# First gathered rows in the places of keys, values and attention probabilities, with two weight blocks loaded there afterwards

## The chip, the cores and the metric

The kernel runs on one core of a Trainium2 chip, in one launch. The metric is the device time of one execution in microseconds (us); the number compared is the median of the runs. The chip's core has a tensor engine (PE), a vector engine (DVE), a scalar engine (ACT), GpSimd (POOL), a sync engine (SP) that only issues transfers here, and 16 DMA engines that carry every transfer, whoever issued it.

## The reference, cut to what matters

Two transformer blocks for 256 tokens of width 1024, in float32. The change lies in the second one, at the seam between its attention and its last part, `peer`: each token picks 16 of 16,384 experts for each of 8 heads, and for each pick one row of `u` and one of `v` (1024 numbers each) is fetched.

```python
def peer(h, w_query, sub_keys, u_tab, v_tab):
    q = rmsnorm((xt @ w_query).reshape(T, PEER_HEADS, 2, PEER_PK_DIM))
    s = jnp.einsum('thpd,pnd->thpn', q, sub_keys)
    s1, i1 = lax.top_k(s[:, :, 0], PEER_TOPK)
    s2, i2 = lax.top_k(s[:, :, 1], PEER_TOPK)
    ...
    best, pos = lax.top_k(cand, PEER_TOPK)
    eidx = jnp.take_along_axis(cidx, pos, axis=-1)
    gate = jax.nn.softmax(best, axis=-1)
    ...
        act = jax.nn.gelu(jnp.einsum('td,thkd->thk', xb, u_tab[ib])) * gb
        return jnp.einsum('thk,thkd->td', act, v_tab[ib])
```

Before it stand, for both halves of 128 tokens, the attention (`diff_attention`, heads by keys and values), the products with `w_branch_attn`, `w_branch_sgu` and `w_out`, and a norm.

## The kernel before, in words

All of on-chip memory that matters is one tensor `AR` with 128 partitions, cut up by hand. `o = W0 + 4096` is an offset in it. From `o` lie the keys `KX` (2048 numbers), from `o + 2048` the values `VX` (2048), from `o + 16384` the probabilities `PP`, and from `o + 18432` further attention scratch (`TT`, `AA` and the start of `ATT`). All four are last used by the last attention product, the event ("mm", "av", 15).

The second block is worked in an order written out by hand, `ORDER`, a list of stages that every engine walks through, each taking the stages that are its own. The first half of the tokens (a = 0) is carried through to `peer` first. Then come 256 "rows": row (ix, k) is the gather of one expert row for each of 128 tokens, 16 rows (k) for each of 16 pairs of half and head (ix). Row number n is 16·ix + k. The rest of the second half's mixer (a = 1) is laid between the rows by the table `late`: after row 12 stage hn1, after row 22 the product `ba` 0 (with `w_branch_attn`, first block), after row 26 `ba` 1 (second block), after rows 34 and 38 `op` 0 and 1 (with `w_out`), then the query products `qm` and the routing (`rt0` to `rt5`) of later heads.

A row goes through four engines. POOL issues the gather (L2128) once the indices of its head are there ("ei", ix) and its place is free. DVE multiplies the first 1024 numbers with the token and sums (L1695). For each pair of rows ACT computes the gate and two diagonal matrices (L2057, L2063). PE multiplies the second 1024 numbers into the sum (L1027, 32 small matmuls for a pair, event ("mm", "row", ix, p)); with that the places of both rows are free. ACT, DVE and PE keep to the order of the list, so a stage that waits holds back the rows behind it.

`row_places()` plans where each row lands. It keeps a list of places of 2048 numbers, takes the first, notes what frees it, and puts it at the end. Ahead of row 0 the list holds the halves of three weight slots (free once `wq` 0, `w_bs` 0 1 and `w_bs` 1 1 have been used) and the place `o + 21504`: seven places, so row n goes where row n - 7 was. More come in at `yt` 1 (after row 30) and later.

SP issues the weight loads in its own part, in order. At the stage `take` 0 it issues the last two blocks of `w_branch_sgu`, the first two of `peer_w_query`, and then, after ("mm", "av", 15), three blocks for the second half of the tokens: `w_branch_attn` 0 at `W0`, `w_branch_attn` 1 at `o` (both key and value places) and `w_out` 0 at `o + 16384`. Each is 2048 KB. The next load on SP after them is `w_out` 1, which waits for the use of `w_branch_attn` 0; the blocks of `peer_w_query` follow.

Of the kernel before, what the change touches and what calls it, by code (L numbers as in the profile page):

```python
# [14 lines left out]
NS = 6  # L15
# [106 lines left out]
def build(nc, D, out):  # L122
    from contextlib import ExitStack
    ctx = ExitStack()
    with ctx:
# [48 lines left out]
        o = W0  # L174
# [10 lines left out]
        o = W0 + 4096  # L185
# [25 lines left out]
        o = W0 + 4096  # L211
# [41 lines left out]
        def weight(name, n):  # L253
            return D[name][n].rearrange("p (j n) -> p j n", j=8)
# [101 lines left out]
        def expert_order():  # L356
            todo, pre = [], 0
            for dc in range(4):
                pieces = [(m, n, q) for m, q in AHEAD[dc] for n in range(2)]
                total, done = len(pieces), 0  # L360
                for b in range(16):
                    if dc < 3:
                        upto = total * (b - 2) // 13 if b > 2 else 0
                    else:
                        upto = (9 * (b - 2) // 5 if b < 8 else 9 + 9 * (b - 7) // 8) if b > 2 else 0
                    here = pieces[done:upto]
                    news = [(m, q) for m, n, q in here if n == 0]
                    if dc < 3:
                        for x in news:
                            todo.append(("pre", pre, *x))  # L370
                            pre += 1
                    todo.append(("down", dc, *divmod(b, 4)))
                    if dc == 3:
                        for x in news:
                            todo.append(("pre", pre, *x))
                            pre += 1
                    if b % 4 == 0 and b + dc:
                        todo.append(("spread", *divmod(4 * dc + b // 4 - 1, 4)))
                    if b == 2 and dc:
                        todo.append(("turn", dc - 1))  # L380
                    todo += [("piece", *x) for x in here]
                    done = upto
                assert done == total
            todo += [("bias",), ("spread", 3, 3), ("biasb",)]
            return todo

        PHASE = expert_order()
        ROWS = {}

        def row_places():  # L390
            halves = [[NARENA + i * SLOT, NARENA + i * SLOT + 2048] for i in RING]
            free = {}
            for i, event in ((2, ("wq", 0, 0)), (0, ("w_bs", 0, 1)), (1, ("w_bs", 1, 1))):
                free.update({k: ("used", *event) for k in halves[i]})
            bufs = list(free)
            for stage, *x in ORDER:
                new = {}
                if (stage, *x) == ("bs", 1, 1):
                    new[o + 21504] = ("zn", 1)
                elif (stage, *x) == ("yt", 1):  # L400
                    new[o + 2048] = ("used", "w_ba", 1, 1)
                elif (stage, *x) == ("qme", 3, 1):
                    new = {k: ("used", "wq", 1, 0) for k in halves[3]}
                elif (stage, *x) == ("rt0", 8):
                    new = {o + 16384: ("used", "wq", 0, 1), o + 18432: ("used", "wq", 0, 1), W0 + 2048: ("used", "wq", 3, 0)}
                free.update(new)
                bufs += new
                if stage == "row":
                    k = bufs.pop(0)
                    ROWS[(*x,)] = k, free[k]  # L410
                    free[k] = ("mm", "row", x[0], x[1] // 2)
                    bufs.append(k)

        row_places()

        def tensor(pe, w):
# [596 lines left out]
            def v_step(ix, p):  # L1015
# [3 lines left out]
                for r in range(2):  # L1019
                    k = 2 * p + r  # L1020
                    off, _ = ROWS[ix, k]
                    w.wait_ge("landed", ix, k)
# [25 lines left out]
            def last_row(k):  # L1048
                off, _ = ROWS[15, k]
                for m in range(2 if k == 12 else 0):  # L1050
                    _, before = banks.use("leave", 1, m)
                    w.wait_ge(*before)
                w.wait_ge("last", k)
                w.wait_ge("landed", 15, k)
                for m in range(2):
                    x = pe.matmul(PS[:, banks.at("leave", 1, m), :], LAST[:, k - 12, :], AR[:, off + 1024 + m * 512:off + 1536 + m * 512],
                                  start=(k == 12), stop=(k == 15), skip_group_check=True)
                    if k == 15:
                        x.then_inc(*w.hit("mm", "leave", 1, m))
# [11 lines left out]
        def vector(v, w):  # L1071
# [617 lines left out]
            def row(ix, k):  # L1689
                a, h = work[ix]  # L1690
                off, _ = ROWS[ix, k]
                rows = AR[:, off:off + 1024]
# [408 lines left out]
        def gpsimd(pool, w):  # L2101
# [22 lines left out]
            def row(ix, k):  # L2124
                off, free = ROWS[ix, k]
                w.wait_ge("ei", ix)
                w.wait_ge(*free)
                pool.indirect_dma_start(out=AR[:, off:off + 2048], out_offset=None, in_=D["peer_uv_2"],  # L2128
                                        in_offset=bass.IndirectOffsetOnAxis(ap=EI[:, ix, k:k + 1], axis=0)).then_inc(
                    *w.hit(f"row{off}", ix, k, also=[("landed", ix, k)], by=16))  # L2130
# [7 lines left out]
        def sync(sp, w):  # L2138
            user, turn, ids = {}, [0], [list(range(NS))]

            def load(slot, key, src, *shape, count=None):
                n = 1
                for s in shape:
                    n *= s
                dst = AR[:, place[slot]:place[slot] + n]
                if len(shape) == 2:
                    dst = dst.rearrange("p (a b) -> p a b", a=shape[0])
                elif len(shape) == 3:
                    dst = dst.rearrange("p (a b c) -> p a b c", a=shape[0], b=shape[1])
                IN[key] = dst  # L2150
                if slot in user:
                    w.wait_ge("used", *user[slot])
                own = COUNT.get(slot, slot) if count is None else count
                sp.dma_start(dst, src).then_inc(*w.hit(f"slot{own}", *key, also=[("in", *key)], by=16))
                user[slot] = key

            def ring(key, src, *shape):
                slot = ids[0][turn[0] % len(ids[0])]
                turn[0] += 1
                load(slot, key, src, *shape)  # L2160
# [83 lines left out]
            for stage, *x in ORDER:  # L2244
                if stage == "rest" and (x[1] == 0 or x[0] not in ("k", "v")):
                    ring(("w_in2", x[0], x[1]), D["w_in_2"][PAIRS.index(x[0]), 3].rearrange("p (n j c) -> p n j c", n=2, j=2), 2, 2, 512)
                elif stage == "zn1" and x[0] == 0:
                    w.wait_ge("mm", "y", 3)
                    load(NS + 2, ("rows",), D["rows"].partition_broadcast(128), 2, 1024)
                elif stage == "bs" and x[1] == 0:  # L2250
                    square(("w_bs", *x), "w_branch_sgu_2", x[0])
                elif stage == "take" and x[0] == 0:
                    for n in range(2):
                        square(("w_bs", n, 1), "w_branch_sgu_2", n)
                    assert turn[0] % 4 == 2
                    for n in range(2):
                        square(("wq", n, 0), "peer_w_query_2", n)
                    w.wait_ge("mm", "av", 15)
                    for slot, key, name, n in ((NS, "w_ba", "w_branch_attn_2", 0), (NS + 4, "w_ba", "w_branch_attn_2", 1),
                                               (NS + 5, "w_op", "w_out_2", 0)):  # L2260
                        load(slot, (key, n, 1), weight(name, n), 8, 512)
                    turn[0], ids[0] = 0, [NS, NS + 5]
                elif stage == "ba" and x[1] == 0:
                    square(("w_ba", *x), "w_branch_attn_2", x[0])
                elif stage == "op" and x != [0, 1]:
                    square(("w_op", *x), "w_out_2", x[0])
                elif stage == "qm" and x in ([4, 0], [6, 0], [0, 1]):
                    square(("wq", x[0] // 2, x[1]), "peer_w_query_2", x[0] // 2)
                elif stage == "leave":
                    a = x[0]  # L2270
                    for m in range(2):
                        f = slice(m * 512, (m + 1) * 512)
                        w.wait_ge("out", a, m)
                        sp.dma_start(out[a * 128:(a + 1) * 128, f], OUTS[a][:, f]).then_inc(*w.hit("stored", a, m, by=16))
# [133 lines left out]
```

## Time and profile before

| | |
|---|---|
| median of 3 runs | 2083.95 us (2083.92 to 2088.63) |
| profiled execution, its own time | 2088.11 us |
| span of the profile | 2086.3 us |
| mean granted clock of the tensor engine | 0.81 |
| PE busy, DVE busy, ACT busy, POOL busy | 71%, 37%, 21%, 15% of the span |
| DMA, whole span | 800.00 MB, 383 GB/s on average |

The busy shares are means over stages with quite different limits. Times below are from the start of the span. The first row is issued at 1402.0 us; what comes before and after is to be read in stretches.

### The profile page before, as it was taken

To read this page: it belongs to the slowest core of one execution; us is meant where nothing else is said; L and a number is where in the kernel's file an instruction comes from. 1 tells how busy PE (TensorE), PEld (TensorE's weight loads), DVE (VectorE), ACT (ScalarE), POOL (GpSimd) and SP (SyncE) were. 2 spreads that over 40 slices of the span, in tenths; PEclk is the share of its full clock that TensorE was granted. 3 is DMA by queue.
4 is the path that set the end of the run, shared out by engine and by line. 5 is a ranking of instruction groups with operands and counts; after the bars stand their busy time and mean duration, and the time that the engine had idled before them with its cause. 6 is when DMAs were issued, how large, how long until landed. Compare 5 with 4: busy or idle time off the path is not lost.

```text
span 2086.3 us, 27127 instructions
## 1 busy us (share of the span) xinstructions
PE 1476.3 (71%) x11468; PEld 647.3 (31%) x11468; DVE 782.1 (37%) x1941; ACT 430.1 (21%) x1013; POOL 304.8 (15%) x290
## 2 busy tenths in 40 slices
PE   9999566877565555689899999986767744444444
PEld 7654122422111112234334445563235410000001
DVE  5832010000000000000122265547767677867764
ACT  1331100000000000011000145643245622221212
POOL 0010000000000000000000000004344444544441
PEclk9999788888878887799999999997788855555556
DMA  9798999999999999999998754469999999999997
GB/s 406 287 404 369 388 428 428 426 429 427 428 427 429 427 428 426 423 406 419 404 414 347 296 187 146 164 261 390 415 422 420 420 420 421 421 421 420 421 421 304
DMA packets 78057, 800.00 MB, mean 383 GB/s; under 512 B 9232, under 2 KB 9360, under 8 KB 10736
## 3 DMA queue, kind: packets, MB, share of 16 engines
q1 hardware_dynamic: 40304, 529.61, 60.9%
q0 software_dynamic: 37632, 268.65, 31.1%
q8 instruction: 91, 1.49, 0.3%
q14 instruction: 30, 0.25, 0.0%
HBM read 796.98 MB, written 1.05 MB: 383 GB/s over the span
## 4 chain that ended last, share of the span: by engine, by line
PE 42%; DMA 41%; DVE 9%; ACT 3%; issue 2%; POOL 2%; SPq 0%; DVEq 0%; ACTq 0%; POOLq 0%
DMA AR<-in_peer_uv,AR 14%; DMA AR<-in_w_gate 10%; DMA AR<-in_w_up 10%; PE PS L811 6%; PE PS L745 6%; DMA AR<-in_w_down 5%; PE PS L443 4%; PE PS L776 4%; DVE AR L1695 3%; PE PS L454 3%; PE PS L891 2%; POOL AR L2128 2%; PE PS L1027 2%; PE PS L984 2%; PE PS L707 1%
## 5 line engine op out<-in xcount | busy, mean ns | idle before, releaser
L745 PE MATMUL PS<-AR 128*32 128x512 f32 x2048 | 316.0, 751 | 200.4 <-DMA AR<-in_w_up 110.8
L1027 PE MATMUL PS<-AR 32*32 32x512 f32 x4032 | 225.5, 931 | 289.8 <-ACT AR L2063 289.7
L2128 POOL DMA_INDIRECT AR<-in_peer_uv,AR x256 | 288.8, 1128 | 967.4 <-DVE AR L1686 665.3
L1695 DVE CUSTOM_DVE_ANT_0 AR<-AR 128x1024 f32<-128x1024 f32 x256 | 309.3, 1222 | 161.7 <-DMA AR<-in_peer_uv,AR 161.3
L1323 DVE TENSOR_TENSOR AR<-AR,PS 128x512 f32<-128x512 f32 x16 | 11.0, 688 | 571.9 <-PE PS L745 571.9
L745 PEld LDWEIGHTS PS<-AR 128*32 128x32 f32 x2048 | 63.6, 124 | 422.7 <-DMA AR<-in_w_up 173.2
L776 PE MATMUL PS<-AR 128*32 128x256 f32 x2048 | 148.1, 439 | 53.5 <-DMA AR<-in_w_down 53.5
L1027 PEld LDWEIGHTS PS<-AR 32*32 32x32 f32 x4032 | 37.4, 125 | 432.6 <-ACT AR L2063 426.9
L811 PE MATMUL PS<-AR 128*128 128x512 f32 x336 | 154.2, 602 | 0.0
L776 PEld LDWEIGHTS PS<-AR 128*32 128x32 f32 x2048 | 68.8, 123 | 139.4 <-DMA AR<-in_w_down 70.0
L443 PE MATMUL PS<-AR 128*128 128x512 f32 x224 | 102.1, 610 | 1.9 <-DVE AR L1093 1.9
L2057 ACT ACTIVATE AR<-AR 128x2 f32<-128x2 f32 x126 | 25.6, 203 | 375.9 <-DVE AR L1695 375.6
L1378 DVE TENSOR_TENSOR AR<-AR,PS 128x512 f32<-128x512 f32 x56 | 38.5, 688 | 145.6 <-PE PS L811 116.8
L2122 POOL MEMSET AR<- 128x378 f32 x1 | 0.4, 412 | 630.3 <-PE PS L745 630.3
L811 PEld LDWEIGHTS PS<-AR 128*128 128x128 f32 x336 | 61.3, 190 | 76.3 <-issue 75.8
L984 PE MATMUL PS<-AR 128*128 128x128 f32 x512 | 69.3, 300 | 5.2 <-DVE AR L1618 3.9
L984 PEld LDWEIGHTS PS<-AR 128*128 128x128 f32 x512 | 66.7, 214 | 11.4 <-issue 5.9
L2063 ACT ACTIVATE AR<-AR 128x32 f32<-128x32 f32 x252 | 67.3, 314 | 8.9
L443 PEld LDWEIGHTS PS<-AR 128*128 128x128 f32 x224 | 42.9, 196 | 57.1 <-issue 57.1
L1351 DVE COPY AR<-PS 128x256 f32<-128x256 f32 x16 | 6.8, 422 | 134.5 <-PE PS L776 134.5
L454 PE MATMUL PS<-AR 128*128 128x256 f32 x256 | 56.3, 381 | 0.5 <-DVE AR L1093 0.5
L1896 ACT COPY AR<-PS 128x512 f32<-128x512 f32 x16 | 9.3, 584 | 222.3 <-PE PS L758 222.3
(320 smaller groups left out, 1592.3 us busy)
## 6 DMA issues: line engine op xcount, KB each, us to landing
AR<-in_w_up SPq DMA_DIRECT2D x64, 2048.0 KB, 17.4
AR<-in_w_down SPq DMA_DIRECT2D x64, 2048.0 KB, 14.5
AR<-in_w_gate SPq DMA_DIRECT2D x63, 2048.0 KB, 20.9
AR<-in_w_in SPq DMA_DIRECT2D x33, 1024.0 KB, 7.4
AR<-in_w_ada SPq DMA_DIRECT2D x12, 2048.0 KB, 13.2
AR<-in_w_out SPq DMA_DIRECT2D x6, 2048.0 KB, 8.9
AR<-in_w_in SPq DMA_DIRECT2D x5, 2048.0 KB, 14.0
AR<-in_peer_w_query SPq DMA_DIRECT2D x5, 2048.0 KB, 11.5
```

The lines of the kernel that those rows point to most:

```text
L443: i = pe.matmul(PS[:, b, :], src[:, j, a * 128:(a + 1) * 128], IN[key][:, j, :], start=(j == 0), stop=(j == 7))
L454: i = pe.matmul(PS[:, b, q * 256:(q + 1) * 256], IN[key][:, j, (e + q) * 128:(e + q + 1) * 128], src[:, j, :], start=(j == 0), stop=(j == 7))
L745: x = pe.matmul(PS[32 * q:32 * q + 32, bk, :], XS[e][:, j, :], src[:, q * 512:(q + 1) * 512], start=(j == 0), stop=(j == 7), skip_group_ch ...
L776: x = pe.matmul(PS[32 * g:32 * g + 32, b, 0:256], HDT[4 * q + g][:, sh, blk * 32:(blk + 1) * 32], IN[key][:, g, sh, :], start=(blk == 0 an ...
L811: x = pe.matmul(PS[:, b, :], HT[:, 2 * q + j, a * 128:(a + 1) * 128], IN[key][:, n, j, :], start=(j == 0), stop=(j == 1))
L891: x = pe.matmul(PS[:, to[n][0], :], HT[:, j, a * 128:(a + 1) * 128], IN[key][:, n, j - 6, :], start=False, stop=(j == 7))
L984: x = pe.matmul(PS[:, b, q * 128:(q + 1) * 128], IN[key][:, j, (2 * r + q) * 128:(2 * r + q + 1) * 128], HT[:, j, a * 128:(a + 1) * 128], ...
L1027: x = pe.matmul(PS[c:c + 32, ACC[a][g], :], DI[t, p, r, :], AR[t, off + 1024 + m * 512:off + 1536 + m * 512], start=(h == 0 and p == 0), s ...
L1378: v.tensor_tensor(d, d, PS[:, banks.at("part", m, n, q, a), :], ADD).then_inc(*w.hit("summed", m, n, q, a, also=[("part", m, n, q, a)]))
L1695: v.tensor_tensor_reduce(rows, rows, HB[:, a, :], 1.0, 0.0, MULT, ADD, DOT[:, ix, k:k + 1]).then_inc(*w.hit("dot", ix, k))
L2063: i = act.activation(DI[:, p, r, :], SG2[:, ix % 2, 2 * p + r, :], ACT.Copy, scale=two[:, r:r + 1])
L2128: pool.indirect_dma_start(out=AR[:, off:off + 2048], out_offset=None, in_=D["peer_uv_2"], in_offset=bass.IndirectOffsetOnAxis(ap=EI[:, ix, ...
```

## The change

The four places of the attention become places for rows, at the head of the list. After the stage hn1 of the second half (behind row 12) they are taken out of the list again, and what frees each of them is noted in `GIVEN`. SP waits for that before it loads `w_branch_attn` 1 at `o` and `w_out` 0 at `o + 16384`; `w_branch_attn` 0, at `W0`, is loaded as before.

```diff
-        ROWS = {}
+        ROWS, GIVEN = {}, {}
 
         def row_places():
             halves = [[NARENA + i * SLOT, NARENA + i * SLOT + 2048] for i in RING]
-            free = {}
+            free = {k: ("mm", "av", 15) for k in (o, o + 2048, o + 16384, o + 18432)}
             for i, event in ((2, ("wq", 0, 0)), (0, ("w_bs", 0, 1)), (1, ("w_bs", 1, 1))):
                 free.update({k: ("used", *event) for k in halves[i]})
             bufs = list(free)
@@
+                for k in (o, o + 2048, o + 16384, o + 18432) if (stage, *x) == ("hn1", 1) else ():
+                    bufs.remove(k)
+                    GIVEN[k] = free.pop(k)
                 free.update(new)
                 bufs += new
@@
                     for slot, key, name, n in ((NS, "w_ba", "w_branch_attn_2", 0), (NS + 4, "w_ba", "w_branch_attn_2", 1),
                                                (NS + 5, "w_op", "w_out_2", 0)):
+                        for k in {NS + 4: (o, o + 2048), NS + 5: (o + 16384, o + 18432)}.get(slot, ()):
+                            w.wait_ge(*GIVEN[k])
                         load(slot, (key, n, 1), weight(name, n), 8, 512)
```

## Rows read from the trace of the kernel before

**Rows 1.** The page: DMA over 40 slices of 52 us, and the gather queue.
```profile
DMA  9798999999999999999998754469999999999997
GB/s 406 287 404 369 388 428 428 426 429 427 428 427 429 427 428 426 423 406 419 404 414 347 296 187 146 164 261 390 415 422 420 420 420 421 421 421 420 421 421 304
...
q0 software_dynamic: 37632, 268.65, 31.1%
```
**Rows 2.** Windows, busy by engine, then PEclk, DMA share, GB/s.
```profile
1510.00:2060.00 550.00, 283.35 (x3977) 108.90 (x3975) 394.18 (x1013) 172.66 (x456) 243.27 (x214) 0.62 1.01 421
```
**Rows 3.** Timeline of DVE near the end: start, duration, idle before and its releaser.
```profile
2065.07 1.23 DVE L1695 CUSTOM_DVE_ANT_0 AR<-AR 128x1024 f32<-128x1024 f32 x1 [1.26 <-DMA AR<-in_peer_uv,AR]
...
2067.54 1.23 DVE L1695 CUSTOM_DVE_ANT_0 AR<-AR 128x1024 f32<-128x1024 f32 x1 [1.24 <-DMA AR<-in_peer_uv,AR]
```
**Rows 4.** Timeline of SP's queue around the start of the rows.
```profile
1385.50 0.80 SPq L2154 DMA_DIRECT2D AR<-in_w_branch_attn  x2
1386.35 0.43 SPq L2154 DMA_DIRECT2D AR<-in_w_out  x1
...
1480.12 0.33 SPq L2154 DMA_DIRECT2D AR<-in_w_out  x1
```
**Rows 5.** Windows around the three weight loads.
```profile
1378.00:1386.00 8.00, 6.83 (x38) 6.33 (x38) 2.95 (x6) 3.16 (x11) 0.00 (x0) 0.79 0.04 18
1386.00:1402.00 16.00, 14.27 (x95) 11.56 (x96) 9.40 (x41) 4.97 (x13) 0.00 (x0) 1.00 0.97 392
```
**Rows 6.** Timeline of POOL: gathers 0, 1, 2, 4, 7, 15 and 19.
```profile
1402.00 1.01 POOL L2128 DMA_INDIRECT AR<-in_peer_uv,AR  x1 [607.56 <-DVE AR L1686]
1403.32 0.97 POOL L2128 DMA_INDIRECT AR<-in_peer_uv,AR  x1 [0.30 <-issue]
1404.92 0.94 POOL L2128 DMA_INDIRECT AR<-in_peer_uv,AR  x1 [0.64 <-PE PS L443]
...
1411.79 0.94 POOL L2128 DMA_INDIRECT AR<-in_peer_uv,AR  x1 [4.69 <-PE PS L443]
...
1417.72 1.49 POOL L2128 DMA_INDIRECT AR<-in_peer_uv,AR  x1 [2.30 <-PE PS L1027]
...
1442.63 1.06 POOL L2128 DMA_INDIRECT AR<-in_peer_uv,AR  x1 [5.02 <-PE PS L1027]
...
1451.67 1.29 POOL L2128 DMA_INDIRECT AR<-in_peer_uv,AR  x1 [1.07 <-PE PS L1027]
```
**Rows 7.** Windows from the first row on.
```profile
1402.00:1412.00 10.00, 9.96 (x27) 4.50 (x25) 2.30 (x6) 6.45 (x10) 4.07 (x5) 1.00 0.83 296
1412.00:1436.00 24.00, 13.03 (x167) 6.88 (x168) 22.87 (x66) 7.32 (x21) 10.08 (x10) 0.72 1.01 422
1436.00:1456.00 20.00, 13.83 (x175) 8.55 (x173) 10.08 (x18) 11.31 (x20) 9.44 (x10) 0.74 0.94 348
...
1470.00:1510.00 40.00, 33.24 (x276) 13.03 (x277) 26.67 (x65) 9.46 (x29) 17.21 (x15) 0.78 1.00 412
```
**Rows 8.** Timeline of DVE: its work on row 0 and on row 22.
```profile
1411.55 0.69 DVE L1515 TENSOR_TENSOR AR<-AR,PS 128x512 f32<-128x512 f32 x1 [5.09 <-PE PS L443]
1412.16 1.22 DVE L1695 CUSTOM_DVE_ANT_0 AR<-AR 128x1024 f32<-128x1024 f32 x1
...
1469.39 1.22 DVE L1695 CUSTOM_DVE_ANT_0 AR<-AR 128x1024 f32<-128x1024 f32 x1
```
**Rows 9.** Timeline of PE: pairs 8/9 and 12/13, then `ba` 0 and 1.
```profile
1435.31 5.83 PE L984 MATMUL PS<-AR 128*128 128x128 f32 x32
1441.06 1.14 PE L1027 MATMUL PS<-AR 32*32 32x512 f32 x32
...
1449.24 2.02 PE L1027 MATMUL PS<-AR 32*32 32x512 f32 x32 [2.14 <-ACT AR L2063]
...
1472.29 7.80 PE L443 MATMUL PS<-AR 128*128 128x512 f32 x16
...
1482.29 7.13 PE L443 MATMUL PS<-AR 128*128 128x512 f32 x16
```
**Rows 10.** Issue to landing: `w_out` at 1386, `w_out` at 1480, both `w_branch_attn`.
```profile
DMA to landing us min/median/max: 17.7/17.7/17.7
DMA to landing us min/median/max: 9.7/9.7/9.7
DMA to landing us min/median/max: 7.5/10.4/13.3
```
**Rows 11.** Windows while rows and weights travel together.
```profile
1520.00:1530.00 10.00, 9.56 (x105) 5.44 (x103) 4.05 (x9) 2.65 (x7) 3.88 (x3) 1.00 1.02 430
```

## The prediction

> **What bounds the kernel now.** I read the page's 40 slices first, for where the transfers have room. They are full or nearly so except around 1200 to 1400 us, where the rate falls to 146 GB/s, and from slice 27 on they are full again to the end [rows 1]. So a byte moved out of that trough into the rows is no longer free; that is what this change has to be asked about.
>
> Second, the windows of the row phase. From 1510 to 2060 us the DMA share is 1.01 at 421 GB/s, DVE is busy for 394 of 550 us, PE for 283 [rows 2]. One row is 268.65 MB / 256 = 1.049 MB [rows 1], which at 421 GB/s is 2.49 us; near the end DVE starts a row every 2.47 us and before each waits 1.2 us for the transfer [rows 3]. The phase is bound by bytes. The end therefore comes when the last row has landed, and that moves only with the bytes that travel behind 1402 us and with the idle time of the DMA engines there.
>
> Third, the seam. SP issues three weight blocks between 1385.5 and 1386.8 [rows 4]. The DMA had been almost idle (share 0.04); from 1386 to 1402 it moves 16 x 392 = 6.27 MB, the three blocks of 2.097 MB [rows 5]. The first gather starts at 1402.0, released by the indices that DVE makes (L1686), not by a place [rows 6]. So the weights fill just the hole before the first row.
>
> Fourth, the windows behind 1402 us, for idle time that more places could fill: 296 GB/s for 10 us, 422 for 24 us, 348 for 20 us, and 412 for 40 us between 1470 and 1510 [rows 7].
>
> **The change part by part.** *Two weight blocks leave the hole.* By the plan there are now 11 places at the start. Rows 0 to 3 take the four of the attention, rows 4 to 9 the halves of the slots, row 10 `o + 21504`; rows 11 and 12 come back to `o` and `o + 2048`. So SP waits for pair 10/11 and pair 12/13; `o + 16384` and `o + 18432` had only rows 2 and 3 and are free long before. Pair 12/13 leaves PE at 1451.3 (start 1449.24) [rows 9]; then both blocks are issued, 65 us later than before. The hole is not filled by anything else: nothing waits behind these loads on SP that could go early, since the next one (`w_out` 1) waits for `ba` 0 and went out at 1480.1 anyway [rows 4], and POOL can't start before its indices. Cost: 2 x 2.097 = 4.19 MB, at the 421 GB/s of the bound phase [rows 2] +9.96 us. If the blocks travel at the 430 GB/s that stood in a stretch with a weight block beside rows [rows 11] it is +9.75. I take +10.0.
>
> By the Trainium skill, page "DMA: Bandwidth & Descriptors", section "Specifications", HBM gives one core about 358 GB/s. By that an estimate of the same term is 11.7 us. The trace does not agree, with 421 GB/s held over 550 us [rows 2].
>
> *First rows, 1402 to 1412 us.* Rows 0 and 1 go out as before. Row 2 waited for `w_bs` 0 1 until 1404.92 and goes 0.3 us earlier, row 4 waited until 1411.79 [rows 6] and goes at about 1407 (the fifth issue, at 1.3 us from one to the next as between the first two [rows 6]). Does it help? By 1412 only 2.96 MB had moved while four rows (4.2 MB) were out, so the queue never ran dry; the low rate is mostly the ramp of the first gathers, which stays. Bounds: nothing, or all of 10 x (421 - 296)/421 = 2.97 us [rows 7]. It is nearest to nothing, as four rows were out either way, but a fuller queue should bring the full rate some 2 us sooner: -0.5 us.
>
> And DVE's first row is not waiting for data: it starts at 1412.16 behind the gating product that PE released (5.09 us of idle there) [rows 8]. From then DVE is busy 22.87 of 24 us [rows 7]. So the four rows that land earlier are not consumed earlier, and places come free from then on as before: 1417.7 is the first [rows 6].
>
> *The gap of 1436 to 1456 us.* Here PE holds the pair 8/9 back behind a query product of 5.83 us until 1441.06 [rows 9], and row 15, which needs that pair's place, goes only at 1442.63 [rows 6]. With the change rows 13 to 19 reach back nine places instead of seven. At 1436, 2.96 + 24 x 0.422 = 13.1 MB or 12.5 rows are in [rows 7], and of the 17 rows to number 16 four and a half are still out: 11 us, which carries to 1447; rows 17 and 18 (released by pair 8/9 at 1442.6) carry to 1452, row 19 to 1454. From row 20 on the list has its seven places again and row 20 waits for pair 12/13 as it did before, but at just that moment the two weight blocks come. Bounds: nothing, or 20 x (421 - 348)/421 = 3.47 us [rows 7]. Mostly filled, with a ragged edge around 1452 where one row is out: -2.9 us.
>
> *1470 to 1510 us.* `ba` 0 and 1 keep PE for 7.80 and 7.13 us [rows 9], which delays places and leaves 412 GB/s [rows 7]. With rows behind by the weights' time more of them are out when PE stops. Bounds: nothing, or 40 x 9/421 = 0.86 us: -0.8.
>
> *The new wait.* `ba` 1 needs its block on PE at 1482.3 [rows 9]. Issued at 1451.5, and taking at most the 17.7 us of the last of three blocks at 1386, or the 9.7 us that `w_out` took among rows [rows 10], it is there by 1469, 13 us early; `w_out` 0 is needed later still. I price the wait at nothing; the cover is those 13 us. While the blocks travel the rows get what is left. The 9.7 us beside a full row queue are 2.1 MB at about 270 GB/s with 2 us of latency, so for some 15 us rows come at 150 GB/s and row 22 lands near 1471, where DVE had worked it at 1469.39 before [rows 8]. That is a shift inside the sum of bytes, not a loss.
>
> The page "DMA: Bandwidth & Descriptors", section "Queues, rings and completion order", in the Trainium skill says that each DMA engine takes turns between its queues, a packet at a time. That is what would let the blocks overtake rows issued before them. The 9.7 us of `w_out` among rows agree [rows 10].
>
> **Sum.** +10.0 - 0.5 - 2.9 - 0.8 = +5.8 us. Against the profiled execution's own 2088.11 us that is 2093.9. That execution lies 4.2 us above the median of the runs; the term is one of bytes and carries over unchanged: 2083.95 + 5.8 = 2089.75, about 0.28% slower.
>
> **The rivals.**
> 1. *Bytes move, gaps are partly filled* (the sum): +3 to +8 us. The bounds are 10.0 - 7.3 = +2.7 and +10. Chance 0.60, about 0.38 of it below +6.25 us.
> 2. *The gaps are not filled.* If they come from ramps and ragged ends of gathers, not from want of places, or if others open while weights and rows share the engines, the full price stands: +8 to +11 us, 2092 to 2095. For it: 1402 to 1412 was slow with four rows out. Against it: row 15 visibly waits for a place for 5.02 us. Chance 0.22.
> 3. *The weights are late for `ba` 1.* It decides if a block takes over 31 us from issue. Then PE stops with all rows behind it; seven rows out cover 17 us of that. Price: +11 to +15 us. The longest landing here is 17.7. Chance 0.04.
> 4. *Faster: the weights find room beside the rows.* If 421 GB/s is what gathers alone can do and the other queue rides on top, the +10.0 falls away, and what remains is the filled gaps, -4.2 us, at most -7.3: 2079.8 to 2076.7. For it: 430 against 421 GB/s with a block in flight. Against it: the share of 1.01 is of all 16 engines, and 9 GB/s of room would take 460 us to carry 4.19 MB. It is over 0.3% faster only if all gaps are filled too. Chance 0.10, of it 0.04 faster by over 0.3%.
> 5. *Nothing much happens*: the hole or the gaps are worth less or more than read, 0 to +3 us. Chance 0.04.
>
> **How the numbers follow.** 0.3% is 6.25 us, about what a measurement of this kernel tells from no change. Faster: 0.04 from rival 4. Within 0.3%: 0.38 + 0.06 + 0.04 = 0.48. Slower: 0.22 + 0.22 + 0.04 = 0.48. The sum lies just inside the bound; the sides are nearly even. The range from +1 to +10.5 us, 2085 to 2094.5, leaves out rivals 3 and most of 4 and the top of 2. The likeliest case's own range is 2087 to 2092.
>
> **What would show it.** Right: one weight block from 1386 to about 1393, then a DMA share near nothing until 1403; 11 gathers issued by 1415.5; DVE's first row still at about 1412; 1436 to 1456 near 421 GB/s; both blocks issued near 1451.5; the last row landing some 6 us later than before with 421 GB/s throughout. Wrong: a rate clearly above 421 while the blocks travel (rival 4), gaps as before or new ones behind 1456 (rival 2), PE idle on `w_branch_attn` before `ba` 1 (rival 3). What would upset all of it is a first gather that starts earlier than 1402, since then the hole would not be empty.

## The result, and the profile after

The changed kernel takes 2091.73 us (median of 7 runs, 2090.7 to 2094.92) against 2083.95. The ratio is 1.0033, 95% interval 1.0019 to 1.0048, so +4.0 to +10.0 us. Run again beside other runs of before it gave 1.0028 (1.0017 to 1.0039). It is slower by about the 5.8 us of the sum; one ratio lies just above the bound of 0.3% and the other just below it.

The profiled execution's span is 2088.9 us (own time 2090.83), only 2.6 us more than the span of before. The two profiles can't be compared by their ends, since their first gathers do not start together: 1397.55 us here, 1402.00 before [rows 6]. In the 13 profiles of this study it lies between 1392.4 and 1402.0, whatever the kernel. So every time below is counted from the first gather of its own profile. From there to DVE's last row is what I call the row phase.

DVE's last row, changed kernel and then before:

```profile
2076.35 1.23 DVE L1698 CUSTOM_DVE_ANT_0 AR<-AR 128x1024 f32<-128x1024 f32 x1 [1.24 <-DMA AR<-in_peer_uv,AR]
```
```profile
2074.94 1.23 DVE L1695 CUSTOM_DVE_ANT_0 AR<-AR 128x1024 f32<-128x1024 f32 x1 [1.23 <-DMA AR<-in_peer_uv,AR]
```

The row phase is 2076.35 - 1397.55 = 678.8 us after and 672.9 before: +5.9 us. The page of the changed kernel, DMA and GB/s over the 40 slices, to be laid beside [rows 1]:

```profile
DMA  9798999999999999999998645359999999999997
GB/s 406 286 404 358 423 427 428 427 427 430 428 427 428 428 427 428 421 401 424 403 420 350 276 181 180 144 196 424 420 422 418 420 421 420 421 421 420 421 421 291
```

The trough is deeper and the slice behind it fuller: 196 and 424 GB/s in slices 27 and 28 where before had 261 and 390. SP's queue in the changed kernel shows why, with what SP waited for:

```profile
1381.03 67.05 SPq L2157 DMA_DIRECT2D AR<-in_w_branch_attn  x2
1448.12 32.31 SPq L2157 DMA_DIRECT2D AR<-in_w_out  x2
```
```profile
SPq L71 <- PE PS L1030: 66.3, 1, 66.3
```

The first block goes out at 1381.0; then SP stands 66.3 us, until pair 12/13 has left PE, and issues the other two 50.2 and 50.6 us behind the first gather. The hole ahead of the rows is now nearly empty (8 GB/s and less), and the stretches from 10 us behind the first gather on are full. Windows of the changed kernel (busy by engine, PEclk, DMA share, GB/s): two in the hole, then from the first gather on in the steps 0 to 10, 10 to 20, 34 to 56, 68 to 80 and 80 to 108 us, and the long rest:

```profile
1388.00:1390.00 2.00, 2.00 (x20) 2.00 (x19) 1.83 (x13) 0.00 (x0) 0.00 (x0) 1.00 0.03 8
...
1394.00:1396.00 2.00, 2.00 (x6) 0.95 (x5) 1.83 (x6) 1.28 (x1) 0.00 (x0) 1.00 0.00 0
...
1397.55:1407.55 10.00, 9.94 (x27) 4.49 (x25) 2.31 (x6) 6.45 (x10) 7.61 (x8) 1.00 0.82 292
1407.55:1417.55 10.00, 3.86 (x67) 1.29 (x68) 9.79 (x32) 1.48 (x6) 4.82 (x5) 0.76 1.01 426
...
1431.55:1453.55 22.00, 15.67 (x207) 9.53 (x205) 12.14 (x30) 12.05 (x23) 6.92 (x8) 0.73 1.02 423
...
1465.55:1477.55 12.00, 7.68 (x43) 2.98 (x44) 9.48 (x26) 4.44 (x10) 1.88 (x2) 0.64 1.01 419
1477.55:1505.55 28.00, 19.33 (x223) 7.57 (x224) 16.33 (x36) 4.74 (x17) 11.37 (x11) 0.93 1.01 423
1505.55:2055.55 550.00, 286.37 (x3984) 110.84 (x3952) 396.69 (x1023) 172.69 (x456) 243.65 (x216) 0.63 1.01 420
```

The same steps in before; the third is the gap around 1442, and 399 is the stop at `ba`:

```profile
1402.00:1412.00 10.00, 9.96 (x27) 4.50 (x25) 2.30 (x6) 6.45 (x10) 4.07 (x5) 1.00 0.83 296
1412.00:1422.00 10.00, 4.71 (x67) 1.32 (x68) 9.79 (x32) 1.47 (x6) 5.54 (x6) 0.68 1.01 424
...
1436.00:1458.00 22.00, 14.79 (x207) 8.79 (x205) 12.04 (x30) 12.05 (x23) 10.36 (x10) 0.76 0.94 353
...
1470.00:1482.00 12.00, 11.67 (x112) 4.40 (x112) 8.69 (x22) 4.82 (x12) 3.02 (x3) 0.85 1.01 399
1482.00:1510.00 28.00, 21.57 (x179) 8.63 (x165) 17.98 (x44) 4.64 (x17) 14.19 (x13) 0.76 1.00 417
```

From 34 to 56 us the rate went from 353 to 423 GB/s: that gap is closed. The first ten us are as slow as they were (292 against 296), though eight gathers are issued in them where before had five (POOL's counts). And the early rows are not used earlier. DVE in the changed kernel, to set against [rows 8]:

```profile
1407.08 0.69 DVE L1518 TENSOR_TENSOR AR<-AR,PS 128x512 f32<-128x512 f32 x1 [5.09 <-PE PS L446]
1407.69 1.22 DVE L1698 CUSTOM_DVE_ANT_0 AR<-AR 128x1024 f32<-128x1024 f32 x1
```

It starts on row 0 at 10.14 us behind the first gather; before it was 10.16, behind the same 5.09 us of waiting for PE.

**A ledger for the row phase.** In each profile I take seven stretches behind the first gather and work out what each fell short of 421 GB/s, as length x (421 - rate)/421. The row phase less the sum of these is my measure of the time that the bytes alone need. The table, in us, is made in this way from the windows and from the times of the first gather and of DVE's last row; "end" is the span behind that last row's start.

```
                     phase    shortfall in stretch                        sum  phase   end
                              0-10 10-20 20-34 34-56 56-68 68-80 80-108        - sum
before               672.9    3.0  -0.1   0.0   3.6  -0.1   0.6   0.3    7.3  665.7  11.4
before, again        673.5    2.8   0.0  -0.1   4.4   0.0   0.5   0.5    8.2  665.3  13.5
changed              678.8    3.1  -0.1   0.0  -0.1   0.0   0.1  -0.1    2.7  676.1  12.6
changed, again       678.3    2.6  -0.1   0.0  -0.2   0.1   0.1  -0.1    2.4  675.9  13.8
delay alone          683.8    2.5   1.0  -0.1   4.0   0.0  -0.1   0.5    7.8  675.9  12.8
blocks out           674.6    2.6   0.9  -0.1   4.2  -0.1   0.7   0.7    8.9  665.8  12.9
blocks out, places   671.7    3.0  -0.1   0.0   0.2   0.1   3.2  -0.1    6.2  665.5  13.7
half                 674.2    2.6  -0.2   0.0   0.4   0.0   0.2   0.5    3.5  670.7  13.3
back early           680.2    2.8  -0.1  -0.1   0.0   0.1   0.0   1.9    4.5  675.7  13.6
three late           684.0    3.0  -0.1   0.0  -0.1  -0.1   0.0  -0.1    2.6  681.4  12.7
query later          669.5    2.6   0.4  -0.1   0.5   0.0   0.3   0.1    3.7  665.8  13.1
query later, again   670.2    3.0   0.0   0.0   0.5   0.0   1.1   0.0    4.4  665.8  13.5
changed, query later 679.4    3.0  -0.1   0.0  -0.1   0.0  -0.1   1.0    3.8  675.6  13.3
```

### The profile page after: what moved, and what is told of

The parts are those of the page before. It is cut to its first block, busy times and chain, and to the rows that moved or that the text cites. A ratio compares the mean times of both kernels' runs of the same rounds, so it can differ in the third digit from the quotient of the medians.

```text
span 2088.9 us, 27128 instructions
## 1 busy us (share of the span) xinstructions
PE 1472.1 (70%) x11468; PEld 644.8 (31%) x11468; DVE 782.7 (37%) x1941; ACT 429.9 (21%) x1013; POOL 299.4 (14%) x290
## 4 chain that ended last, share of the span: by engine, by line
DMA 42%; PE 41%; DVE 9%; ACT 3%; issue 2%; POOL 2%; SPq 0%; DVEq 0%; ACTq 0%; POOLq 0%
DMA AR<-in_peer_uv,AR 15%; DMA AR<-in_w_up 11%; DMA AR<-in_w_down 8%; DMA AR<-in_w_gate 8%; PE PS L814 6%; PE PS L748 6%; PE PS L446 4%; PE PS L779 4%; DVE AR L1698 3%; PE PS L457 3%; PE PS L894 2%; PE PS L1030 2%; POOL AR L2131 2%; PE PS L710 1%; PE PS L568 1%
## 5 line engine op out<-in xcount | busy, mean ns | idle before, releaser
L748 PE MATMUL PS<-AR 128*32 128x512 f32 x2048 | 321.8, 763 | 197.5 <-DMA AR<-in_w_up 108.4
L2131 POOL DMA_INDIRECT AR<-in_peer_uv,AR x256 | 283.4, 1107 | 976.2 <-DVE AR L1689 662.8
L779 PE MATMUL PS<-AR 128*32 128x256 f32 x2048 | 143.7, 429 | 56.5 <-DMA AR<-in_w_down 56.5
```

What stands on the lines that cost most here:

```text
L748: x = pe.matmul(PS[32 * q:32 * q + 32, bk, :], XS[e][:, j, :], src[:, q * 512:(q + 1) * 512], start=(j == 0), stop=(j == 7), skip_group_ch ...
L779: x = pe.matmul(PS[32 * g:32 * g + 32, b, 0:256], HDT[4 * q + g][:, sh, blk * 32:(blk + 1) * 32], IN[key][:, g, sh, :], start=(blk == 0 an ...
```

## The experiments

**The delay alone** (e1_late_only): seven places as before, the blocks held back.

```diff
+                        if slot != NS:
+                            w.wait_ge("mm", "row", 0, 6)
                         load(slot, (key, n, 1), weight(name, n), 8, 512)
```

> The list of places as before (seven), but the two weight blocks are loaded only once pair 12/13 has left. Bytes theory: 4.19 MB behind the first row cost 10.0 us at 421 GB/s; only the idle time behind 1451 us can be filled by the blocks themselves (0.8 us up to 1456, 0.9 us from 1470 to 1510), the gap around 1442 stays. So +8 us on the median and +8.3 us from the first gather to the last row's work. Rival, the extra places are what costs (rows and weights in each other's way), not the late bytes: near 0 to +3 us.

Measured: ratio 1.0058 (1.0044 to 1.0071), +12 us. The row phase is 683.8 us, 10.6 above the mean of the two profiles of before (673.2). Windows in the steps 0 to 10 and 34 to 56:

```profile
1399.03:1409.03 10.00, 9.94 (x27) 4.49 (x25) 2.31 (x6) 6.44 (x10) 4.08 (x5) 1.00 0.83 315
1433.03:1455.03 22.00, 14.82 (x208) 8.99 (x207) 12.05 (x31) 12.04 (x23) 12.09 (x10) 0.77 0.93 345
```

The gap of 34 to 56 stays (345 GB/s), as the sum of bytes and gaps (the "bytes theory" of the expectations) had it, but the total is 2.3 us more than I expected in the row phase, and more on the median. The ledger has it as shortfall: 1.0 us lost between 10 and 20, where before lost nothing, and the 0.8 us of the gap of 34 to 56 that the blocks should have filled is not filled (4.0 us lost). The rival (0 to +3) is out: late bytes alone cost the full price.

**Without the blocks, with seven and with eleven places** (e2_blocks_out, e3_blocks_out_places). In both the two blocks aren't loaded, and their products do not wait for them. The diff is that against before; the one against the changed kernel has the same lines.

```diff
-                        load(slot, (key, n, 1), weight(name, n), 8, 512)
+                        if slot == NS:
+                            load(slot, (key, n, 1), weight(name, n), 8, 512)
+                        else:
+                            IN[key, n, 1] = ar(place[slot], 8, 512)
+                            user[slot] = (key, n, 1)
...
-                w.wait_ge("in", *key)
+                if key not in (("w_ba", 1, 1), ("w_op", 0, 1)):
+                    w.wait_ge("in", *key)
```

> The kernel before, with the two weight blocks (w_branch_attn 1 and w_out 0 of the second half) not loaded at all; their products read what lies in those places, so the second half's numbers are not the reference's. Bytes theory: the blocks lay in a hole that nothing else uses, so leaving them out gives 0 us, within 0.5 us from the first gather to the last row. Rival, the first gathers were slow between 1402 and 1412 because the tail of the blocks (landed 1404) was in the way: up to -1.6 us.

Measured: ratio 1.0002 (0.9991 to 1.0013). In the hole the blocks cost nothing that the median shows. The row phase is 674.6 us, 1.4 above the mean of before, where I had said within 0.5: 0.9 us are lost between 10 and 20. The time of the bytes is 665.8 us, as in before.

> The changed kernel with the two weight blocks not loaded (products as in the run that leaves them out of the kernel before). This prices the places alone. Bytes theory: the filled gaps, 3.5 us (1436 to 1456) and 0.9 us (1470 to 1510), with nothing from the first 10 us: -3.5 to -4.4 us against before, and 10 us less than the changed kernel. Rival, extra places help nothing and the gaps are of another making: 0 us.

Measured: ratio 1.0000 (0.9988 to 1.0011). This expectation failed: no gain on the median. Windows of the kernel with eleven places in the steps 34 to 56 and 68 to 80, then two of its gathers:

```profile
1435.06:1457.06 22.00, 14.91 (x207) 8.77 (x205) 13.33 (x32) 12.05 (x23) 8.05 (x9) 0.77 1.01 417
1469.06:1481.06 12.00, 12.00 (x98) 4.91 (x83) 7.69 (x18) 3.26 (x9) 3.83 (x4) 0.85 0.87 309
```
```profile
1469.61 0.94 POOL L2132 DMA_INDIRECT AR<-in_peer_uv,AR  x1 [5.01 <-PE PS L1031]
...
1479.52 0.94 POOL L2132 DMA_INDIRECT AR<-in_peer_uv,AR  x1 [7.02 <-PE PS L1031]
```

The gap of 34 to 56 is closed (417 against 353 GB/s), and 3.2 us are lost a little later instead. By then the list has its seven places again, the rows are ahead, and `ba` 0 holds PE for some 9 us, so POOL waits 7.02 us for a place and the rows in flight run out. The places alone hand the gap on. The median shows nothing of it; the row phase is 1.5 us shorter than in before. Against the changed kernel the row phase is 7.1 us shorter: 10.6 us of bytes less 3.5 us of shortfall, nearly all of it the 3.2 us that the late blocks cover in the changed kernel.

**Half of the change** (e4_half): only the two places at `o + 16384` and `o + 18432`.

```diff
-            free = {k: ("mm", "av", 15) for k in (o, o + 2048, o + 16384, o + 18432)}
+            free = {k: ("mm", "av", 15) for k in (o + 16384, o + 18432)}
...
-                for k in (o, o + 2048, o + 16384, o + 18432) if (stage, *x) == ("hn1", 1) else ():
+                for k in (o + 16384, o + 18432) if (stage, *x) == ("hn1", 1) else ():
...
-                        for k in {NS + 4: (o, o + 2048), NS + 5: (o + 16384, o + 18432)}.get(slot, ()):
+                        for k in {NS + 5: (o + 16384, o + 18432)}.get(slot, ()):
```

> Only the two places of the probabilities and scratch become row places (nine at the start); only w_out 0 is loaded late, w_branch_attn 1 stays in the hole. Bytes theory: +5.0 us for 2.10 MB, less 3 to 4.3 us of gaps filled: +0.7 to +2 us. Rival, the cost hangs on a wait for the late block and not on its bytes: as the changed kernel, +7 us, or nothing.

Measured: ratio 1.0010 (0.9998 to 1.0021), +2 us; row phase 674.2, +1.0 on the mean of before. Two more places close the gap of 34 to 56 as well as four do (0.4 us left), for half of the bytes.

**The places given back at once** (e6_back_early).

```diff
-                for k in (o, o + 2048, o + 16384, o + 18432) if (stage, *x) == ("hn1", 1) else ():
+                for k in (o, o + 2048, o + 16384, o + 18432) if (stage, *x) == ("row", 0, 4) else ():
```

> The four places serve rows 0 to 3 only and go back to the blocks at once: SP waits for pairs 0/1 and 2/3, so the blocks are issued near 19 us behind the first gather instead of 50. Bytes theory: the same 4.19 MB behind the first row, and rows put back by them, so that the stop of PE around 34 to 56 us is covered too: +5 to +7 us against before, as the changed kernel. Rival, it is places at that moment that fill the gap: there are seven again, so 3.5 us of it come back and it is +9 to +11 us.

Measured: ratio 1.0034 (1.0021 to 1.0047), +7 us; row phase 680.2. Windows in the steps 34 to 56 and 80 to 108:

```profile
1429.34:1451.34 22.00, 13.94 (x169) 8.20 (x170) 12.27 (x25) 12.72 (x25) 6.55 (x7) 0.66 1.01 422
...
1475.34:1503.34 28.00, 20.07 (x201) 8.07 (x199) 15.23 (x29) 4.99 (x19) 13.79 (x12) 0.93 0.97 393
```

From 34 to 56 nothing is lost, with seven places at that moment, so the rival is out: two blocks issued at 16 and 19 us fill this gap as well as four more places do. In the changed kernel itself it is the places that fill its first 16 us, since the blocks go out only at 50 us; the eleven places without the blocks lose 0.2 us there, the late blocks without the places 4.0. What early blocks do not cover is the stop at `ba`: from 80 to 108 us 1.9 us are lost (393 GB/s), where the changed kernel loses none. That is about the 1.6 us by which this row phase is longer than the changed kernel's. Otherwise it matters little when the blocks are issued behind the first row.

**A third block late** (e7_three_late).

```diff
-                        for k in {NS + 4: (o, o + 2048), NS + 5: (o + 16384, o + 18432)}.get(slot, ()):
+                        for k in {NS: (o, o + 2048), NS + 4: (o, o + 2048), NS + 5: (o + 16384, o + 18432)}.get(slot, ()):
```

> The changed kernel with the third block, w_branch_attn 0 at W0, held back as well until pair 12/13 has left; places as in the change. Bytes theory: 2.10 MB more behind the first row, no gap left to fill with them: +5.0 us on the changed kernel, +12 to +13 us on before, 683.8 us from the first gather to the last row. Rival, the bytes of blocks are partly free beside rows: +0 to +2 us on the changed kernel.

Measured: ratio 1.0058 (1.0046 to 1.0070), +12 us; row phase 684.0 against 683.8 expected. With it the ledger's last column but one has four doses: 665.6 us without a late block (mean of six profiles), 670.7 with one, 675.8 with two (mean of five), 681.4 with three. The first two blocks of 2.10 MB cost 5.1 us each and the third 5.6, and none of it is free beside the rows. The packets counted in the traces say the same: between the first gather and DVE's last row 278.1 to 278.2 MB start in the six profiles, 280.2 MB with one late block, 282.3 with two and 284.4 with three, and from 108 us on, up to 15 us before that last row, the rate is 420.3 to 420.6 GB/s in all 13.

**A version with no byte moved** (e8_query_later). The gap of 34 to 56 begins because a query product stands in front of pair 8/9 on PE. It is moved behind that pair, in the kernel before, and with it, by two rows, the stages that use its result.

```diff
-            for n, *x in ((5, 2, 0), (8, 3, 0), (40, 4, 0), ...
+            for n, *x in ((5, 2, 0), (10, 3, 0), (40, 4, 0), ...
```

> The kernel before with one edit of its order: the query product of head 3 stands after row 10 instead of after row 8, so that pair 8/9 leaves PE ahead of it; blocks in the hole, seven places. Bytes theory: the 3.5 us lost between 34 and 56 us behind the first gather come from rows that wait for pair 8/9, so part of it is won with no byte moved: -1 to -3 us against before, 670 to 672 us from the first gather to the last row. Rival, the stop is only handed on to the next pair, or the win is given back at the product with w_branch_attn as the places alone gave it back: 0.

Measured: ratio 0.9989 (0.9978 to 1.0000); row phase 669.5. The window of 34 to 56, and the gather of row 15, which needs that pair's place:

```profile
1431.70:1453.70 22.00, 15.99 (x208) 8.74 (x176) 14.74 (x34) 10.77 (x22) 12.85 (x12) 0.66 1.01 412
```
```profile
1433.98 0.94 POOL L2128 DMA_INDIRECT AR<-in_peer_uv,AR  x1 [0.65 <-PE PS L1027]
```

The row phase is a little shorter than the 670 to 672 us expected. Row 15 goes 36.3 us behind the first gather; in before it was 40.6 [rows 6]. Repeated:

> The kernel before with the query product of head 3 after row 10, again, since the first verdict lay at the edge of its interval. -2.4 us on the median again, 669.5 us from the first gather to the last row within 1.5. Rival, the first was chance: 0 and 673.

Measured: ratio 0.9981 (0.9968 to 0.9994); row phase 670.2. Both profiles are 2.7 to 4.0 us shorter than those of before. Its ratio is below that of both kernels: against before the gain is 0.1 to 0.2%, where the first interval ends at 1.0000 and the second at 0.9994.

**The same edit on the changed kernel** (e11_change_query_later), same diff on the changed file.

> The changed kernel with the same edit of the order. Bytes theory: the changed kernel has no gap left to fill, so the edit that gave 3.4 us on before gives nothing here: 678 to 679 us from the first gather to the last row, +4 to +8 us against before. Rival, the edit shortens the row phase by itself (less waiting of DVE and ACT): 675 us and 3 us less than the changed kernel.

Measured: ratio 1.0031 (1.0019 to 1.0042); row phase 679.4. What gave some 3 us on before gives nothing where no gap is left, and the rival (675 us) is out: the edit works through the gap.

**Both kernels once more** (e0_change_again, e9_before_again), unedited.

> The changed kernel once more, for a second profile. Bytes theory: from the first gather to DVE's last row 678.8 us again, within 1.5 us, and 420 GB/s or more in every stretch from 10 us behind the first gather; the time behind the last row (12.55 us in the first profile against 11.36 before) varies with the moment at which the tensor engine's clock rises, in either kernel. Rival, the change itself lengthens the end: 12.5 us or more each time and never 11.4.

> The kernel before once more, for a second profile and as a null: 0 us on the median. Bytes theory: 673 to 675 us from the first gather to the last row's work, the stretch from 34 to 56 us behind the first gather again 3.5 to 4.3 us short. The time behind the last row: 12.6 to 13.8 us as in nine other profiles, if the 11.36 of the first profile was chance; 11.4 again if it belongs to this kernel.

Measured: 678.3 us and a ratio of 1.0028 (1.0017 to 1.0039) for the changed kernel, 673.5 us and 0.9998 (0.9986 to 1.0011) for before. The end behind the last row is 13.8 and 13.5 us. The rival of the first, that the change lengthens the end, is out: the 11.4 us of the first profile of before was chance. What varies are eight matmuls on PE that fold the partial sums, and with them the tensor engine's granted clock: they take 4.28 and 6.46 us in the two profiles of before at a mean clock of 0.86 and 0.57, and 5.51 and 6.73 us in those of the changed kernel at 0.66 and 0.54. Timeline of PE, before (first profile) and then the changed kernel (first profile):

```profile
2069.76 4.28 PE L1056 MATMUL PS<-AR 128*128 128x512 f32 x8 [0.52 <-ACT AR L2072]
```
```profile
2071.16 5.51 PE L1059 MATMUL PS<-AR 128*128 128x512 f32 x8 [0.52 <-ACT AR L2075]
```

## Why the prediction was right

The time, 2091.73, is within the range, 1.98 us above the point. Step by step:

- *The bound.* Right. 421 GB/s in before and 420 in the changed kernel over the 550 us behind the seam, and DVE waiting for the last rows, in both kernels.
- *Two blocks leave the hole: +10.0.* Right: without its shortfalls the row phase grew by 10.4 us in the first pair of profiles, and with one, two and three late blocks it is 5.1, 5.1 and 5.3 us a block. 2.10 MB at 421 GB/s are 4.98; where the 0.1 to 0.3 us a block beyond that go was not settled. The estimate of 11.7 us from the 358 GB/s of the Trainium skill (page "DMA: Bandwidth & Descriptors", section "Specifications") would have been too high; the one core that runs here held 420 to 421.
- *Nothing else fills the hole.* Right, 0 to 8 GB/s there. The first gather does not move by the change, and leaving the blocks out altogether gave 1.0002.
- *First rows: -0.5.* Wrong in size. The shortfall of the first 10 us is 2.5 to 3.1 us in all 13 profiles, with seven places or eleven. The term is 0. That a fuller queue brings the full rate sooner is what was wrong: in windows of 1 us before moves 33, 139, 172 and 434 GB/s and the changed kernel 0, 98, 188 and 393, so more than two of the three lost us lie in the first 3 us, when only three gathers have been issued in either. That the term would be near nothing was argued; that DVE does not use the rows sooner was right to 0.02 us.
- *The gap at 1436: -2.9.* Right in kind, under-sized: closed entirely, 3.6 us in that profile of before and 4.4 in the other. The ragged edge that I allowed for isn't there.
- *1470 to 1510: -0.8.* Right, -1.0. But the reason carries more than I gave it. The places alone would have given their 3.5 us back at `ba` (3.2 us lost). That they did not in the changed kernel is the late blocks' doing. I had put the first gap down to places and the second to bytes. Either closes the first, as the blocks issued early show; the second stays open when the blocks go out early (1.9 us lost).
- *The new wait on PE: nothing.* Right. The blocks were issued 50.2 and 50.6 us behind the first gather. Issue to landing, `w_branch_attn` 1 and `w_out` 0 of the changed kernel:

```profile
DMA to landing us min/median/max: 12.3/12.3/12.3
```
```profile
DMA to landing us min/median/max: 19.3/19.3/19.3
```

So the first, issued at 1447.8, was there at 1460.1, and `ba` 1 starts at 1482.29, 22 us later. The second took 1.6 us more than the longest landing of before.

The reading behind this step was wrong, though its outcome was not. The `w_out` that landed in 9.7 us did not travel beside a full row queue: while it travelled, from 1481 to 1486, the rows' queue moved 82, 41, 0, 0 and 8 GB/s, since `ba` 0 had held PE and with it their places. So those 9.7 us do not show that queues take turns. The changed kernel does: from 1452 to 1463, with transfers waiting in both queues, the rows moved 141 GB/s and the blocks 280, in 189 packets of 8 KB against 188 of 16 KB. The number of packets is shared evenly and the bytes are not. The 150 GB/s for 15 us that I gave the rows came out.

- *The sum, +5.8.* The row phase gives +5.9 in the first pair of profiles and +5.3 between the means of two. That it comes so near is in part luck: the bytes cost 0.4 us more than forecast and the first rows gave 0.5 less, while the first gap gave 0.8 more and the second 0.2. The medians differ by 7.8 us in the first comparison and by 4.4 in the second, the ratios by 6.9 and 5.8; neither interval can tell these apart. The end behind the last row was 1.2 us shorter in before's first profile than in the changed kernel's, by chance, which is no part of the change.

Of the rivals, unfilled gaps and full price are what the delay alone shows (+12 us), but not the change. Late blocks did not occur. Blocks free beside rows is excluded by the doses, and 0 to +3 us by the first interval. Slower and within 0.3% were given even chances, and that is where two comparisons left it.

## What to carry to other kernels

Before moving a load, ask which resource is idle at the old place and at the new one. Here 4.2 MB left a stretch in which the DMA engines had nothing else to do, and came back in one that ended with the last byte; the gaps that they helped to close were worth less than half of the price. A gap in transfers that comes from a late buffer is closed more cheaply by freeing that buffer sooner, in the order of the engine that holds it: one product moved behind one pair took some 3 us off the row phase. And more buffers for a while can hand a gap on to the next stop, as the eleven places did without the blocks.

## What the runs showed that I had not expected

The first 10 us of gathers run at 292 to 315 GB/s however many are issued (five to eight) and whether the queue before them is full or empty; about 2.8 us are lost there.

Without the two blocks ahead and with seven places, the stretch 10 to 20 us behind the first gather also falls short:

```profile
1402.38:1412.38 10.00, 3.89 (x67) 1.32 (x68) 9.76 (x32) 1.47 (x6) 5.12 (x6) 0.76 0.97 385
```

It is 385 GB/s there and 378 with the delay alone, against 424 and 420 in before. It is seen only where the fifth gather waits for its place until 9.8 us, once even with the blocks ahead (405 in the first run with the query product later), and in no kernel that has more places for the first rows. Why was not settled. It is not that all rows issued had moved: 15 us behind the first gather seven gathers, 7.3 MB, were issued in the kernel without the blocks and 5.0 MB had moved. It is 1 us of what the four places give the changed kernel over the delay alone.

From one execution to the next, before and changed kernel alike, the first gather moves by up to 10 us (1392.4 to 1402.0) and the end behind the last row by 2.4 us (11.4 to 13.8), while the row phase repeats within 0.7 us for each of the three kernels that were profiled twice. A change of a few us at this place is seen in the phase that it touches long before the median shows it.
